# Router logits with tokens on the partitions, and a narrow expert slot first

## The chip, the cores and the metric

The kernel runs on one core of one Trainium2 chip. The metric is the time of one execution on the device in microseconds (us), the median of several runs. Lower is better.

## The reference, cut to what matters

Two layers over 256 tokens of width 1024, in fp32. What the change touches is the end: the output projection of the second layer's attention, the norm, the router and eight experts, of which each token uses two.

```python
x = x + mixer_c(...)                       # ends in o @ w_o
h = rms_norm(x, od_ffn_norm)
logits = h @ router                        # 1024 x 8
top_vals, top_idx = lax.top_k(logits, 2)
w = softmax(top_vals)
for e in range(8):
    out = out + gates[:, e:e+1] * ((silu(h @ e_gate[e]) * (h @ e_up[e])) @ e_down[e])
x = x + out
```

Each expert has three matrices of 1024 x 3584 (or turned) in fp32, 44 MB; all eight are read, 352 MB of the 419 MB that the kernel reads from HBM. 512 pairs of token and expert fall on eight experts. By the reference's inputs the counts are 60, 48, 76, 45, 100, 74, 52, 57.

## The kernel before

The instructions of each engine are written in order by hand, one block for each of PE, ACT, DVE, POOL (GpSimd) and SP, and the engines meet at semaphores.

**Slots.** The expert stage is a sequence of slots, one expert in each. A wide slot takes up to 128 tokens (`CAP`), a narrow one up to 64 (`CAP_N`). The slots run wide, narrow, wide, narrow and so on, eight in all. The first is always expert 0, so that its weights can be loaded before the router has spoken. Of the others, the three with most tokens go into wide slots. An expert with more tokens than its slot holds gets spare slots, added in pairs of wide and narrow, up to `OVER` pairs (`over` is read into registers by all engines).

**Wide slot** (`wide`, 84 quarters of a weight piece each of [128, 1024]). Each quarter is split in two: ACT writes the high part as fp32r (L1379), DVE the rest (L1958), and PE does three fp32r matmuls (`three`, L999 to L1001) for each 512 columns. Splits run four quarters ahead (`AHEAD`). 56 quarters are gate and up, 28 down. Where gate and up meet down, DVE multiplies the two (L1991) and PE turns the hidden values (L880). Toward the end PE turns the next slot's gathered rows (L916).

**Narrow slot** (`narrow`). PE reads the fp32 weights as they lie in the ring, in two column halves of the array (`both`, L932, each matmul recorded as two). Gate and up take 16 pieces, down 8; no splits. Then turns (L926) and turn rows (L852).

**Weights.** SP loads them in pieces of 1.835 MB, 24 to an expert (8 gate, 8 up, 8 down), into a ring of eight places. A place is loaded again when its piece was split (wide, `lo_ready`) or used (narrow, `n_used`). The first piece of the first narrow slot goes to a ninth place, `beside`. The first eight pieces of expert 0 are loaded during the last part of the attention, and then x is stored to `out`.

**Router** (`experts_pe`, `experts_act`, `experts_dve`). The second half of x is complete when DVE has added the last output-projection block (L2123). PE turns x (L1050, L808), ACT and DVE make a gained split transpose (L1324, L1845). PE forms the logits, 8 rows by 256 tokens, in three fp32r passes; DVE copies them out (L1879) and PE turns them (L817). DVE finds the top two (L1890 to L1903), PE counts with triangular and full matrices of ones (L825 to L829), DVE writes the one-hot of expert 0, PE forms its rows already turned (`first_rows`, L838), and ACT and DVE take them over. `idle_matmuls` stand between. The gained rows h are made by DVE (L1859) and stored to `h_rows` by ACT.

**From slot to slot.** During a slot DVE writes the next expert's one-hot, PE turns it into row numbers (`place`, L846), POOL gathers the rows (`exchange`), and after the slot POOL scatters the results, adding to `out`. Before its first exchange POOL sorts the experts into slots (`by_slot`), sets up the spare slots in a loop over `OVER` (L2579 to L2598) and signals `spare_ready`; SP waits for that before it loads a second expert.

Of the kernel before, what the change touches and what calls it, by code (L numbers as in the profile page):

```python
# [54 lines left out]
OVER = 3  # L55
# [24 lines left out]
T_BANK = (6, 7)  # L80
N_BLOCKS = ((0, 512), (512, 512), (1024, 512), (1536, 256))
# [183 lines left out]
def trunk(nc, a, out):  # L265
# [14 lines left out]
    with ExitStack() as ctx:  # L280
# [309 lines left out]
        logitsT = y[0:N_EXP, NW:NW + SEQ]  # L590
        logits_done = sem("logits_done")
        logits_copied = sem("logits_copied")
# [3 lines left out]
        route_ready = sem("route_ready")  # L596
        gain_row_loaded = sem("gain_row_loaded")
# [43 lines left out]
        def is_beside(s, i):  # L641

            return s[0] is None and s[1] == 0 and i == 0
# [11 lines left out]
        def opening(s):  # L655

            return s[0] is None and s[1] == 0

# [16 lines left out]
        def _(sp):  # L675
# [64 lines left out]
            def load_narrow(s):  # L740

                e = sp.value_load(ids[0:1, bass.ds(upto(s, 2, 1), 1)], min_val=0, max_val=N_EXP - 1)
                for i in range(E_PIECES):
                    if is_beside(s, i):
                        load(e, i, beside[:, :], beside_arrived)
                        continue
                    if i < E_RING:
                        sp.wait_ge(lo_ready, upto(s, EQ, split_of_piece(E_PIECES - E_RING + i)))
                    elif is_beside(s, i - E_RING):
                        sp.wait_ge(lo_ready, split_of_piece(E_PIECES - E_RING))  # L750
# [15 lines left out]
            over = sp.value_load(ids[0:1, OVER_AT:OVER_AT + 1], min_val=0, max_val=OVER)  # L766
            sp.wait_ge(spare_ready, 1)
            last = over + (PAIRS - 1)
            for pair in range(PLAIN):
# [14 lines left out]
        def late_bank(k):  # L784

            return bank[(2, 3, 0, 5)[k - KD // 2]]

        def experts_pe(pe, three, turn_norm):
# [7 lines left out]
            def logits(k):  # L796

                pe.wait_ge(hT_lo_ready, 3 * KD + k + 1)
                es = slice(k * N_EXP, (k + 1) * N_EXP)
                return three(bank[4][0:N_EXP, 0:SEQ], aT_hi[:, 0, es], aT_lo[:, 0, es], hT_hi[:, k, :], hT_lo[:, k, :],  # L800
                             k == 0, k == KD - 1)

            for k in range(KD // 2):
                logits(k)
            for t in range(TB):
# [1032 lines left out]
        def experts_dve(dve, projection, split_to, link):  # L1838
# [35 lines left out]
            for k in range(KD):  # L1874
                low(k)
# [783 lines left out]
```

## Time and profile before

| | before |
|---|---|
| median of 3 runs | 1277.42 us (1277.34 to 1278.24) |
| profiled execution | 1278.76 us, span 1276.9 us |
| PE busy | 1216.0 us (95%) |
| DVE, ACT busy | 725.7 us (57%), 663.3 us (52%) |
| read from HBM | 419.06 MB, 332 GB/s over the span |
| mean granted clock of PE | 0.991 of 2.4 GHz |

The span goes from the first to the last instruction. A busy PE is not PE at its peak, as matmuls are pipelined. The expert stage takes the last two thirds of the span. In the chain of work that ended last, PE has 48% and the DMA 11%.

### The profile page before, as it was taken

To read this page: it belongs to the slowest core of one execution; us is meant where nothing else is said; L and a number is where in the kernel's file an instruction comes from. 1 tells how busy PE (TensorE), PEld (TensorE's weight loads), DVE (VectorE), ACT (ScalarE), POOL (GpSimd) and SP (SyncE) were. 2 spreads that over 40 slices of the span, in tenths; PEclk is the share of its full clock that TensorE was granted. 3 is DMA by queue.
4 is the path that set the end of the run, shared out by engine and by line. 5 is a ranking of instruction groups with operands and counts; after the bars stand their busy time and mean duration, and the time that the engine had idled before them with its cause. 6 is when DMAs were issued, how large, how long until landed. Compare 5 with 4: busy or idle time off the path is not lost.

```text
span 1276.9 us, 15629 instructions
## 1 busy us (share of the span) xinstructions
PE 1216.0 (95%) x5885; PEld 842.9 (66%) x5885; DVE 725.7 (57%) x1065; ACT 663.3 (52%) x964; POOL 153.6 (12%) x228
## 2 busy tenths in 40 slices
PE   9989999999989999999899999889999988999997
PEld 7757888888767787843388773348875326878432
DVE  4976555546876889910189950048992007899000
ACT  5676544445796787710278750048772016877100
POOL 0400000000460598010000000010000000000000
PEclk9999999999999999999999999999999998999999
DMA  9804953410635899999999999999999999999995
GB/s 339 308 20 173 357 194 132 149 62 25 247 149 202 314 387 378 363 376 426 427 420 425 428 423 416 426 419 428 427 425 406 428 425 421 426 427 413 389 428 219
DMA packets 62070, 422.98 MB, mean 331 GB/s; under 512 B 5217, under 2 KB 12556, under 8 KB 37420
## 3 DMA queue, kind: packets, MB, share of 16 engines
q1 hardware_dynamic: 59456, 416.40, 80.0%
q0 software_dynamic: 2224, 4.51, 1.5%
q8 instruction: 47, 0.77, 0.2%
q10 hardware_dynamic: 316, 1.07, 0.2%
q14 instruction: 27, 0.22, 0.0%
HBM read 419.06 MB, written 5.24 MB: 332 GB/s over the span
## 4 chain that ended last, share of the span: by engine, by line
PE 48%; DMA 11%; issue 6%; DVE 5%; ACT 1%; POOL 0%; POOLq 0%; SPq 0%; DVEq 0%; ACTq 0%
PE bank L999 12%; PE bank L1001 11%; PE bank L1000 11%; PE bank L932 11%; DMA ring<-in_od_e_gate_dram 7%; DMA ring<-in_od_e_down_dram 4%; DVE w_lo L1958 2%; DVE flat L1991 1%; PE bank L880 1%; DVE aT_lo L1978 0%; DMA out_dram<-h,idx_t 0%; ACT w_hi L1379 0%; PE bank L846 0%; PE bank L838 0%; PE bank L1218 0%
## 5 line engine op out<-in xcount | busy, mean ns | idle before, releaser
L1958 DVE TENSOR_TENSOR w_lo<-ring,w_hi 128x1024 fp32r<-128x1024 f32 x268 | 320.0, 1224 | 54.4 <-ACT w_hi L1379 48.1
L1379 ACT ACTIVATE w_hi<-ring 128x1024 fp32r<-128x1024 f32 x268 | 279.1, 1060 | 81.0 <-PE bank L1001 48.7
L932 PE MATMUL bank<-ring,flat 128*64 128x512 f32 (+1 forms) x1456 | 305.2, 572 | 16.6 <-DMA ring<-in_od_e_down_dram 13.3
L999 PE MATMUL bank<-w_hi,hT_hi 128*128 128x512 f32 (+3 forms) x728 | 282.5, 388 | 11.2 <-DVE w_lo L1958 9.2
L1001 PE MATMUL bank<-w_lo,hT_hi 128*128 128x512 f32 (+3 forms) x728 | 278.3, 382 | 0.0
L1000 PE MATMUL bank<-w_hi,hT_lo 128*128 128x512 f32 (+3 forms) x728 | 278.2, 382 | 0.0
L932 PEld LDWEIGHTS bank<-ring,flat 128*64 128x64 f32 x1456 | 99.0, 135 | 205.5 <-issue 163.4
L2074 DVE TENSOR_TENSOR w_lo<-ring,w_hi 128x1024 fp32r<-128x1024 f32 (+3 forms) x124 | 140.4, 1142 | 83.9 <-ACT w_hi L1491 83.7
L999 PEld LDWEIGHTS bank<-w_hi,hT_hi 128*128 128x128 f32 x728 | 138.4, 190 | 41.2 <-issue 11.0
L1491 ACT ACTIVATE w_hi<-ring 128x1024 fp32r<-128x1024 f32 (+3 forms) x124 | 121.0, 987 | 79.3 <-PE bank L1001 74.9
L1001 PEld LDWEIGHTS bank<-w_lo,hT_hi 128*128 128x128 f32 x728 | 138.2, 190 | 26.4
L1000 PEld LDWEIGHTS bank<-w_hi,hT_lo 128*128 128x128 f32 x728 | 138.5, 190 | 24.8
L999 PE MATMUL bank<-w_hi,aT_hi 128*128 128x512 f32 x306 | 122.3, 400 | 3.2 <-DVE aT_lo L1978 1.8
L1001 PE MATMUL bank<-w_lo,aT_hi 128*128 128x512 f32 x306 | 119.6, 391 | 0.0
L1000 PE MATMUL bank<-w_hi,aT_lo 128*128 128x512 f32 x306 | 119.2, 390 | 0.0
L1434 ACT ACTIVATE flat<-bank 128x512 f32<-128x512 f32 (+1 forms) x16 | 8.7, 544 | 186.6 <-PE bank L926 186.6
L1958 DVE TENSOR_TENSOR hT_lo<-ring,hT_hi 128x1024 fp32r<-128x1024 f32 x64 | 78.2, 1222 | 5.3 <-ACT hT_hi L1379 3.5
L2028 DVE SCALAR_TENSOR_TENSOR flat<-bank,gates,flat 128x512 f32<-128x512 f32 (+1 forms) x16 | 10.5, 682 | 119.1 <-PE bank L932 118.3
L1379 ACT ACTIVATE hT_hi<-ring 128x1024 fp32r<-128x1024 f32 x64 | 67.9, 1060 | 9.7 <-PE bank L1001 9.7
L2611 POOL TENSOR_TENSOR gates<-g_cols 128x1 f32<-128x1 f32 x8 | 3.4, 427 | 557.4 <-ACT h L1419 293.9
L999 PEld LDWEIGHTS bank<-w_hi,aT_hi 128*128 128x128 f32 x306 | 57.6, 188 | 18.3 <-DVE aT_lo L1978 3.8
L1935 DVE TENSOR_TENSOR hT_lo<-bank,hT_hi 128x512 fp32r<-128x512 f32 x10 | 6.5, 686 | 105.7 <-ACT hT_hi L1366 105.7
(363 smaller groups left out, 1216.8 us busy)
## 6 DMA issues: line engine op xcount, KB each, us to landing
ring<-in_od_e_up_dram SPq DMA_DIRECT2D x64, 1792.0 KB, 18.5
ring<-in_od_e_down_dram SPq DMA_DIRECT2D x64, 1792.0 KB, 23.7
ring<-in_od_e_gate_dram SPq DMA_DIRECT2D x63, 1792.0 KB, 17.6
ring<-in_ev_w_gate_dram SPq DMA_DIRECT2D x5, 2048.0 KB, 9.1
ring<-in_ev_w_up_dram SPq DMA_DIRECT2D x5, 2048.0 KB, 13.4
ring<-in_ev_w_down_dram SPq DMA_DIRECT2D x5, 2048.0 KB, 7.6
ring<-in_ev_w_in_dram SPq DMA_DIRECT2D x8, 512.0 KB, 8.7
ring<-in_ev_w_in_dram SPq DMA_DIRECT2D x2, 2048.0 KB, 15.5
```

What stands on the lines that cost most here:

```text
L880: mm = pe.transpose(bank[T_BANK[g % 2]][:, b * P:(b + 1) * P], ye_act[:, at + r:at + HALF_K * P:HALF_K], ident)
L932: mm = pe.matmul(dst[g * CAP_N:(g + 1) * CAP_N, 0:n], left, rights[g], start=first, stop=final)
L999: pe.matmul(dst, hi, whi, start=first, stop=False)
L1000: pe.matmul(dst, lo, whi, start=False, stop=False)
L1001: return pe.matmul(dst, hi, wlo, start=False, stop=final)
L1379: act.activation(e_hi_at[place_of(n)], eights(e_quarter(n)), ACT.Copy).then_inc(hi_ready, 1)
L1434: act.activation(n_actT[:, first * P:(first + tiles) * P], bank[N_T_BANK[g % 2]][:, 0:tiles * P], ACT.Copy).then_inc(n_actT_ready, 1)
L1491: act.activation(w_hi[:, q % SPLITS, 0:m], ring[:, p["place"], at:at + m], ACT.Copy)\
L1958: dve.tensor_tensor(e_lo_at[place_of(n)], eights(e_quarter(n)), e_hi_at[place_of(n)].bitcast(F32), ALU.subtract).then_inc(lo_ready, 1)
L1991: dve.scalar_tensor_tensor(ye_act[:, at], bank[U_BANK[b]][:, :], rinv_cur, ye_act[:, at], ALU.mult, ALU.mult).then_inc(e_hidden, 1)
L2028: dve.scalar_tensor_tensor(n_act[:, at:at + n], bank[4 + b][:, 0:n], rinv_cur, n_act[:, at:at + n], ALU.mult, ALU.mult).then_inc(n_hidden, 1)
L2074: dve.tensor_tensor(w_lo[:, q % SPLITS, 0:m], ring[:, p["place"], at:at + m], w_hi[:, q % SPLITS, 0:m].bitcast(F32), ALU.subtract).then_in ...
```

## The change

Two things. First, the router: the logits are formed with tokens on the partitions, as plain fp32 matmuls of turned x against a router whose rows were multiplied by the gain beforehand (`router_gained`, DVE), so nothing has to be split or turned back. The last block of the output projection is done token block by token block (`o_last_quarter`), with the add and the turning of each behind it. The second half of h is multiplied by the gain on POOL. Some idle matmuls go.

Second, the order of slots: narrow (expert 0), wide, wide, narrow, wide, narrow, wide, narrow. Expert 0 now has the lowest key in the sorting, so the four others with most tokens are wide. `first_rows` forms 64 columns. `beside` now holds piece 8 of the first slot and is loaded once the logits are done. The first wide slot has PSUM banks of its own (`FIRST_BANKS`) and splits four quarters ahead into the second, which waits for `y_ready` before its second quarter. The expert numbers get a signal of their own, `ids_ready`. The spare slots are computed behind POOL's first exchange, with `OVER` 4 and three instructions more in each.

```diff
-OVER = 3
+OVER = 4
+FIRST_BANKS = ((0, 1, 2, 4, 3, 5, 6), (7, 0, 1, 2, 4, 3, 5), (0, 1), (6, 7))
...
         def is_beside(s, i):
-            return s[0] is None and s[1] == 0 and i == 0
+            return s[0] is None and s[1] == 0 and i == E_RING
+        def per_step(s, narrow, more, unit=1):
+            if opening(s):
+                return unit * (more + (0 if narrow else 1))
+            return upto(s, 2 * unit, unit * (more + (1 if narrow else 0)))
...
+                elif i == E_RING:
+                    sp.wait_ge(logits_done, 1)
+                    load(0, i, beside[:, :], beside_arrived)
+                    continue
                 else:
-                    sp.wait_ge(lo_ready, split_of_piece(i - E_RING))
+                    sp.wait_ge(n_used, 1 if i == 2 * E_RING else i - E_RING + 1)
...
+            def load_first_wides():
+                for n in range(2):
+                    e = sp.value_load(ids[0:1, 2 * n:2 * n + 1], min_val=0, max_val=N_EXP - 1)
+                    for i in range(E_PIECES):
+                        if i >= E_RING:
+                            sp.wait_ge(lo_ready, n * EQ + split_of_piece(i - E_RING))
+                        elif n == 0:
+                            sp.wait_ge(n_used, E_PIECES - E_RING + i + 1)
+                        else:
+                            sp.wait_ge(lo_ready, split_of_piece(E_PIECES - E_RING + i))
+                        load(e, i, e_ring(i), e_arrived[i % E_RING])
...
+            sp.wait_ge(ids_ready, 1)
+            load_first_wides()
             sp.wait_ge(spare_ready, 1)
-            for pair in range(PLAIN):
+            for pair in range(1, PLAIN):
...
+            def turn_late(t):
+                pe.wait_ge(hT_hi_ready, 3 * KD + 2)
                 pe.wait_ge(x_added, X_ADDS[3] - TB + t + 1)
                 for k in range(KD // 2, KD):
+                    at = (k - KD // 2) % (4 if t == 0 else 2) * P
+                    b = 2 if t == 0 else (3, 0)[(k - KD // 2) // 2]
+                    mm = pe.transpose(bank[b][:, at:at + P], xres[:, t, k * P:(k + 1) * P], ident)
+                mm.then_inc(hT_turned, 1)
+            def logits(t, ks):
+                for k in ks:
+                    mm = pe.matmul(bank[4][:, SEQ + t * N_EXP:SEQ + (t + 1) * N_EXP],
+                                   xT_all[:, k, t * P:(t + 1) * P],
+                                   router_gained[:, k * N_EXP:(k + 1) * N_EXP], start=(k == 0), stop=(k == KD - 1))
+                return mm
+            turn_late(0)
+            pe.wait_ge(router_ready, 1)
+            logits(0, first_half)
+            turn_late(1)
+            pe.wait_ge(hT_hi_ready, 3 * KD + 3)
+            logits(0, last_half)
+            logits(1, first_half)
+            pe.wait_ge(hT_hi_ready, 3 * KD + 4)
+            pe.wait_ge(hT_lo_ready, 3 * KD + 1)
+            logits(1, last_half).then_inc(logits_done, 1)
-            idle_matmuls(3)
...
-            idle_matmuls(6)
+            idle_matmuls(4)
...
+                        mm = pe.matmul(bank[N_FIRST_BANKS[k // 4]][:, (k % 4) * CAP_N:(k % 4 + 1) * CAP_N],
+                                       h[:, t, k * P:(k + 1) * P], oh[:, t, 0:CAP_N], start=(t == 0), stop=(t == 1))
...
+                    if n == 1 and s[0] is None and s[1] == 1:
+                        pe.wait_ge(y_ready, 2)
...
+                    if i == 2 and opening(s):
+                        pe.wait_ge(slot_ready, 1)
+                        place()
+                    if i == 13 and opening(s):
+                        pe.wait_ge(n_silu, 4)
+                        pe.wait_ge(slot_ready, 2)
+                        place(place_bank(s, True))
...
             first_rows()
+            narrow((None, 0))
             wide((None, 0))
+            wide((None, 1))
...
+                for t in range(TB):
+                    for k in (k0, k0 + 1):
+                        mm = three(o_bank(j, t)[:, :], hT_hi[:, k, rows], hT_lo[:, k, rows], ...)
+                    mm.then_inc(quarter_used if t == TB - 1 else o_block, 1)
...
+            for t in range(TB):
+                pool.wait_ge(x_added, X_ADDS[3] - TB + t + 1)
+                o = pool.tensor_tensor(h[:, t, NW:], xres[:, t, NW:], acf[:, NW:D], ALU.mult)
+            o.then_inc(h_ready, 1)
...
+            pool.tensor_copy(ids[0:1, 0:N_EXP], ids_f[0:1, 0:N_EXP]).then_inc(ids_ready, 1)
...
+            narrow((None, 0))
+            spares()
             wide((None, 0))
+            wide((None, 1))
```

## Rows read from the trace of the kernel before

**Rows 1.** The page, 40 equal slices of the span: throughput of the DMA

```profile
GB/s 339 308 20 173 357 194 132 149 62 25 247 149 202 314 387 378 363 376 426 427 420 425 428 423 416 426 419 428 427 425 406 428 425 421 426 427 413 389 428 219
```

**Rows 2.** Stages: length, busy PE, PEld, DVE, ACT, POOL; clock, DMA share, GB/s

```profile
404.00:428.00 24.00, 20.84 (x125) 16.04 (x125) 14.91 (x48) 15.64 (x33) 1.55 (x2) 1.00 0.98 393
428.00:432.00 4.00, 4.00 (x25) 3.50 (x25) 3.04 (x6) 2.70 (x4) 1.13 (x4) 1.00 0.07 28
432.00:550.00 118.00, 116.73 (x531) 96.20 (x530) 106.24 (x113) 88.64 (x94) 69.56 (x79) 1.00 0.93 364
...
640.00:750.00 110.00, 108.72 (x492) 89.45 (x491) 99.54 (x97) 86.27 (x92) 1.90 (x3) 1.00 1.01 424
```

**Rows 3.** The chain of waits in the expert stage: start us, us, what

```profile
550.74 19.07 PE bank L932 x96
...
570.35 31.68 PE bank L932 x160
602.03 0.70 PE bank L926 x4
602.75 0.61 ACT flat L1434
...
608.17 25.66 DMA ring<-in_od_e_gate_dram
...
636.31 0.47 PE bank L999
...
742.59 0.44 PE bank L916 x4
...
758.99 19.07 PE bank L932 x96
...
848.58 0.76 PE bank L999
```

**Rows 4.** The chain of waits through the router

```profile
412.40 1.28 DVE flat L2123 x2
...
418.58 1.13 DVE w_lo L1852
...
420.47 0.18 DVE route L1890
...
423.01 0.39 PE bank L825 x2
...
424.30 1.47 PE bank L793 x6
425.77 3.57 PE bank L838 x32
429.34 0.30 PE bank L999
```

**Rows 5.** SP's issues of weight pieces behind the first wide slot: start, length, count

```profile
516.13 30.91 SPq L725 DMA_DIRECT2D ring<-in_od_e_gate_dram  x7
```

**Rows 6.** PE by time in the last narrow slot

```profile
1241.21 6.23 PE L932 MATMUL bank<-ring,flat 128*64 128x512 f32 x28
...
1262.40 1.09 PE L852 MATMUL bank<-cst,h 128*128 128x128 f32 x8
```

**Rows 7.** POOL: a group by line (busy, mean ns), then instructions by time

```profile
L2475 POOL TENSOR_TENSOR ring<-ring,rinv 128x512 f32<-128x512 f32 x2 | 4.0, 2032 | 37.1 <-DVE rinv L2161 37.1
...
433.49 12.64 POOL L2555 TENSOR_TENSOR kr<-cnt,cst 128x32 f32<-128x32 f32 x2 [4.22 <-DVE ids L1954]
...
460.56 1.08 POOL L2579 TENSOR_TENSOR route<-route,cnt 128x16 f32<-128x16 f32 x1
...
467.80 0.19 POOL L2586 COPY pos_t<-cst 128x2 f32<-128x2 f32 x1
...
507.13 0.18 POOL L2608 TENSOR_TENSOR gates<-g_cols 128x1 f32<-128x1 f32 x1
...
564.95 0.18 POOL L2617 TENSOR_TENSOR idx_t<-idx_t 128x1 uint32<-128x1 uint32 x1 [10.37 <-DMA out_dram<-h,idx_t]
```

More of the change, by code:

```diff
@@ L867, in quarter @@
                         half = slice(k % 8 * P, (k % 8 + 1) * P)
-                        mm = three(out(D_BANK[b]), eT_hi[:, half], eT_lo[:, half], wh, wl, k == 0, k == 2 * HALF_K - 1)
+                        mm = three(out(d_bank[b]), eT_hi[:, half], eT_lo[:, half], wh, wl, k == 0, k == 2 * HALF_K - 1)
                     else:
-                        mm = three(out((G_BANK if kind == "gate" else U_BANK)[b]), hT_hi[:, k, 0:CAP], hT_lo[:, k, 0:CAP],
+                        mm = three(out((g_bank if kind == "gate" else u_bank)[b]), hT_hi[:, k, 0:CAP], hT_lo[:, k, 0:CAP],
                                    wh, wl, k == 0, b in ended_banks(kind, n))
@@ L984, in experts_pe @@
             last = over + (PAIRS - 1)
-            for pair in range(PLAIN):
+            for pair in range(1, PLAIN):
                 narrow((None, pair))
@@ L1361, in experts_act, with take_gathered @@
             o.then_inc(e_once, 1)
-            def take_gathered(first):
+            def take_gathered(first, banks):
                 for m in range(2):
@@ L1452, in experts_act @@
             last = over + (PAIRS - 1)
-            for pair in range(PLAIN):
+            for pair in range(1, PLAIN):
                 narrow((None, pair), (None, pair + 1))
@@ L1985, in wide @@
                         split(s, n + AHEAD)
+                    if n + AHEAD >= EQ and opening(s):
+                        split((None, 1), n + AHEAD - EQ)
                     if ended:
@@ L2033, in narrow @@
                         split(after, n)
+            dve.wait_ge(placed, 1)
+            take_halves_placed()
+            narrow((None, 0), (None, 0))
             wide((None, 0))
+            wide((None, 1))
             dve.wait_ge(route_ready, 1)
@@ L2038, in experts_dve @@
             last = over + (PAIRS - 1)
-            for pair in range(PLAIN):
+            for pair in range(1, PLAIN):
                 narrow((None, pair), (None, pair + 1))
@@ L2608, in exchange @@
+            def exchange(s, narrow, dst, rows, to, results):
+                pool.wait_ge(idx_ready, per_step(s, narrow, 2))
+                pool.wait_ge(rows_turned, per_step(s, narrow, 1, 2))
                 pool.tensor_tensor(seen_rows, g_cols[:, 0:1], g_cols[:, 0:1], ALU.add)
                 gather(dst, rows)
[L2610 removed]
+                pool.wait_ge(y_ready, per_step(s, narrow, 1))
                 pool.tensor_tensor(seen_y, g_cols[:, 0:1], g_cols[:, 0:1], ALU.add)
@@ L2614, in exchange @@
                     .then_inc(scattered, 16)
-                pool.wait_ge(gathered, upto(s, 32, 16 * (slot + 1)))
-                pool.wait_ge(scattered, upto(s, 32, 16 * (slot + 1)))
+                pool.wait_ge(gathered, per_step(s, narrow, 1, 16))
+                pool.wait_ge(scattered, per_step(s, narrow, 1, 16))
                 pool.tensor_tensor(idx_cur, idx_next, zero_u, ALU.add).then_inc(idx_taken, 1)
             def wide(s):
-                exchange(s, 0, he[:, 0:NW], h_halves, out[0], ye)
+                if opening(s):
+                    exchange(s, False, he, h_rows, out[0], ye)
+                else:
+                    exchange(s, False, he[:, 0:NW], h_halves, out[0], ye)
             def narrow(s):
-                exchange(s, 1, he, h_rows, out_halves, ye[:, 0:NW])
+                exchange(s, True, he, h_rows, out_halves, ye[:, 0:NW])
             last = over + (PAIRS - 1)
+            narrow((None, 0))
+            spares()
             wide((None, 0))
-            for pair in range(PLAIN):
+            wide((None, 1))
+            for pair in range(1, PLAIN):
                 narrow((None, pair))
```

393 lines of the change are left out of this document (203 added, 190 removed).

## The prediction

> **What bounds the kernel now.** I read the throughput of the DMA by slices first [rows 1]. From the nineteenth slice on (575 us) they move 406 to 428 GB/s, save one of 389 and the last; in the five before (415 to 575) it is 314 to 387. So the expert stage streams weights at a ceiling, except in its first 150 us. Then I cut it into stages [rows 2]. In the 118 us of the first wide slot (432 to 550) the DMA engines are busy for 0.93 and move 364 GB/s; in the later wide slot (640 to 750) 1.01 and 424 GB/s. Just before the stage, from 404 to 428, they run at 393 GB/s to fill the ring, and from 428 to 432 they stand nearly still (28 GB/s): the ring of eight pieces is full and nobody has emptied a place.
>
> The chain of waits gives the slots [rows 3]. Narrow slot: PE begins at 550.74, does gate and up in 19.07 + 31.68 us, and at its end waits 25.66 us for a gate piece. The next wide slot begins at 636.31 and ends at 758.99 (122.7 us); the one after begins at 848.58. A pair, wide and narrow, thus takes 212.3 us for 48 pieces of 1.835 MB: 4.42 us a piece, including the gathers and scatters. The first wide slot runs from 429.34 [rows 4] to 550.74, 121.4 us. So a wide slot consumes a piece in 5.1 us, slower than the DMA delivers, and a narrow slot could consume one in 3.4 us (below). In the steady state the wide slot's surplus of 19 us is eaten by the narrow slot and the DMA sets the pace. At the start it isn't: the ring is full, the wide slot doesn't empty it fast enough, and the issues on SP's queue come every 5.1 us [rows 5], the splits' pace.
>
> The page "DMA: Bandwidth & Descriptors" of the Trainium skill (Where 436 GB/s comes from) says that loads from HBM are bound at about 358 GB/s, below the fabric's 435. By that a piece would take 5.13 us, a wide slot would never fall behind the DMA, and the order of slots would bring nothing. This trace disagrees: 424 GB/s over 110 us [rows 2]. The sums below use the 4.42 us.
>
> **The change, part by part.**
>
> *Router.* Before, DVE adds the two halves of x at 412.40; its routing starts at 420.47, 8.07 us later; from there the first wide slot is 8.87 us away [rows 4]. After, DVE adds token block 0 under the matmuls of block 1, so one add (0.64) remains after 412.4, and transposes of four blocks cost 0.5 (eight of 128x128 took 1.09 [rows 6]). Logits become fp32 matmuls with 8 columns; the nearest row is the count matmul, 0.22 us each for 5 of them between 423.01 and 424.30 with the first at 0.39 [rows 4]. PE: transposes to 412.85, four logits matmuls to 413.75, transposes of block 1 to 414.2, eight more to 416.0 over the copies on ACT and DVE (a copy of 512 columns on ACT took 0.61 [rows 3], these have half), the last four to 416.9. The hT_lo passes, the first split (1.13) on DVE, the copy and the transposes of the logits leave the path. Routing starts at 417.0: 3.5 us gained. With matmuls at 0.39 instead of 0.22 it would be about 1 us later by the last four alone and about 2.5 by all; without any wait between, 0.5 earlier. I take 3.5.
>
> From routing to the first product: 2.54 for the masks and 1.3 for the counts stay. The idle matmuls after them go from six (1.47) to four (1.0): 0.5 gained. DVE's compares, which fitted under six, must fit under 1.0; if they don't, at most the 0.5 comes back. The gained half of h moves from DVE to POOL: two products of 128x512. POOL's nearest rows take 2.0 us [rows 7]; 412.4 + 0.64 + 2 x 2.0 is 417, against 420 when the compares need it. Hidden; if it weren't, each us is a us. First rows stay 16 products in 3.57 with half the columns: the count matmuls with 8 columns also take 0.22, so the width brings nothing (upper gain 1.8). The first slot begins at 429.34 - 3.5 - 0.5 = 425.3.
>
> *DMA at the start.* The piece `beside` (index 8) is issued once the logits are done, at about 417. The five gate pieces, x and h keep the DMA busy to 428 [rows 2]; the ninth piece extends that to 432.3. SP then waits for two used pieces. A narrow slot's gate piece takes 50.75/16 = 3.17 us, so that is 425.3 + 6.3 = 431.6: the DMA has at most 2 us of gap. From about 433.8 piece k lands at 433.8 + 4.42 (k - 8).
>
> *First narrow slot.* Gate and up 50.75; two placements 1.1 (0.54 each, from 550.74 + 19.07 to 570.35 [rows 3]); down 112 recorded matmuls at 6.23/28 = 0.2225 [rows 6], 24.9; turning 14 blocks at 0.70 for four, 2.5; the copy of the first turned ones 0.6 [rows 3]; turn rows 1.1. Sum 81.0: to 506.3. Arrival: piece 23 is due at 500.1 and used from about 503, so PE isn't starved, by 3 us. Piece 24 lands at 504.5; with the 2.5 us from landing to first product (608.17 + 25.66 to 636.31) the wide slot can begin at 507.0. I take 507.0.
>
> *Two wide slots.* Each 121.4, as the first of before (its splits were ahead too; the other row is 122.7). Between them PE needs the first slot's results copied out of two banks, after one quarter (1.4 us) of work; two copies of 0.6 on ACT. I take 0.5 us; nothing if the copies win, 4 if the split pipeline must restart. W2 ends at 507.0 + 121.4 + 0.5 + 121.4 = 750.3. The ring fills again: piece 72 would land at 716.7, and its place comes free 82 us into the slot at about 711, so for the last 40 us of W2 the DMA is held to 5.1 us a piece, just as before at the end of its first wide slot.
>
> *Rest.* From the end of W2 everything is as after the first wide slot of before: 85.57 us to the next wide slot (550.74 to 636.31), at 835.9. There the ring had one piece more (`beside`), but SP waited for two used pieces instead of one; that cancels within 1 us. Before, the same wide slot (the third) began at 848.58. Gain 12.7; with 0.7 us from the earlier reissue of the first freed place, 13.4. What follows is unchanged and bound by the DMA.
>
> *POOL and the queues.* The spare computation leaves the start and comes after the first scatter. In the trace the three spares take 39.3 us (467.80 to 507.13) plus 7.2 of preparation [rows 7]. Four with two or three more instructions each: about 15 us x 4 + 7 = 67. The scatter is over 14.2 us after a slot's end (550.74 to 564.95), so the spares run from 520 to 587, and the gather lands at 597. PE wants it 106 us into W1 (742.59 less 636.31) = 613. Hidden by 16 us. SP's wide loads wait for `ids_ready` at 476; even with the 12.64 us that the first two instructions took in the trace it is there by 456. The splits that stood ahead of the first slot are done during the narrow slot, where DVE has nothing else.
>
> **Sum.** 1276.9 - 13.4 = 1263.5 for the span; with the 1.9 us between span and time of the profiled run (1278.76) 1265.4. The profiled run lay 1.34 above the median 1277.42, so the forecast for the median is 1264.0.
>
> **Rivals.**
>
> *A, as forecast*, chance 0.68: 1260 to 1268.
>
> *B, narrow slot starved*, 0.14: the DMA is less than 3 us ahead of PE in the first narrow slot. If it starts late or the narrow slot takes the 85.57 us of every later one, W1 begins 4 to 8 us later, and nothing gives that back, since two PE-bound slots follow: 1268 to 1272. For it: the deliveries late in narrow slots do lag. Against it: there the ring started nearly empty.
>
> *C, the clock*, 0.06: three idle matmuls go and six become four. The granted clock was 1.00 throughout 404 to 428 in spite of 3.2 us of idle PE in that window [rows 2]. If it fell to half for the first rows (3.57 more) and the first us of the slot, 4 to 6 us: 1268 to 1270.
>
> *D, no gain*, 0.05: both A's PE chain and the DMA lose, by a restart of the splits between the wide slots (4), a starved narrow slot (5) and a router no earlier (4). 1277.
>
> *E, slower*, 0.04: the spares on POOL. They have 16 us of slack; each instruction waits its turn with DVE. If they take t us more than 67, the gather stalls W1 by t - 16 and W2 after it. From t = 32 the change is slower than before; at twice the time (134), 51 us stall, 1264 + 51 = 1315. Against it: DVE was as busy when the three took 13.1 each. The page "SBUF — State Buffer" of the Trainium skill (Who interferes with whom) says that a DVE instruction with two SBUF inputs and a GpSimd one that reads SBUF block each other for a whole instruction. The first wide slot bore about 70 of them in 121.4 us, no more than the 122.7 of one without.
>
> *F, it doesn't do what it says*, 0.03: the first slot is narrow whatever the load. With over 64 tokens on expert 0 a spare pair is added, 212 us: 1476. The reference's inputs give expert 0 sixty tokens, and the smallest gap between second and third logit (0.003) is far above fp32 error; the four other slots hold.
>
> **Range and chances.** The ends take A and B and the unknown costs: below, first rows at half the width (1.8), no waits between logits (0.5) and a shorter narrow slot, 1259; above, B, 1272. Less than 0.2 lies outside. A measurement tells 0.2% (2.6 us) from no change. Faster takes A, B, C and small parts of D: 0.89; same 0.05; slower 0.06.
>
> **What would show it.** Routing starts near 417; the first product on a ring piece near 425; the wide slots at about 507 and 628, narrow at 750, wide at 836. DMA above 415 GB/s from 433 to 710, then about 370 to 750. In the first narrow slot no wait for a down piece over 2 us; W1 without a wait for `gathered`. The prediction is wrong if the time from 425 to W1 is over 85 us, if the second wide slot starts with a gap, or if the gather of W1 lands after 613.

## The result, and the profile after

| | before | after |
|---|---|---|
| median, lowest and highest of 20 runs | 1277.57 (1276.69 to 1279.69) us | 1270.2 (1267.9 to 1279.42) us |
| ratio to before, 95% interval | | 0.995 (0.9939 to 0.9961) |
| span of the profiled execution | 1276.9 us | 1269.6 us |

The change is faster by 7.4 us by the medians (0.6%) and by 6.4 by the ratio (0.5%). The forecast was 1264.0 us, a gain of 13.4, so about half of it came. The median lies inside the stated 1259 to 1272, but above the 1260 to 1268 of the forecast's own case A and in the stretch that was given to rivals B (a starved narrow slot) and C (the clock). The span came out 6.1 us above its forecast of 1263.5. The changed kernel also scatters more: 11.5 us between its lowest and highest run, against 3.0 before.

The throughput of the DMA in 40 slices, on the page of the changed kernel, answers to [rows 1]:

```profile
GB/s 336 310 25 165 366 199 133 149 63 25 222 177 169 376 428 425 420 427 427 426 415 401 357 338 416 427 419 428 427 427 414 428 427 420 427 426 421 395 427 220
```

The five weak slices from 415 to 575 us have become one (376). The hole is not gone: three slices of 401, 357 and 338 stand from 667 to 762 us, at the end of the second wide slot. The same by stages, as [rows 2] (length, busy PE, PEld, DVE, ACT, POOL; granted clock, DMA share, GB/s):

```profile
414.00:416.00 2.00, 2.00 (x18) 2.00 (x17) 0.65 (x4) 1.91 (x7) 0.62 (x5) 0.83 1.02 437
416.00:418.00 2.00, 2.00 (x9) 1.98 (x10) 0.21 (x2) 1.66 (x3) 0.00 (x0) 0.50 1.07 445
418.00:420.00 2.00, 2.00 (x6) 1.53 (x5) 1.73 (x11) 0.00 (x0) 0.00 (x0) 0.50 0.93 389
420.00:422.00 2.00, 2.00 (x8) 1.61 (x7) 0.42 (x3) 0.00 (x0) 0.00 (x0) 0.50 1.07 440
422.00:424.00 2.00, 2.00 (x13) 1.59 (x13) 0.88 (x8) 0.05 (x1) 0.00 (x0) 0.96 0.98 411
432.00:434.00 2.00, 2.00 (x14) 0.69 (x12) 0.00 (x0) 0.00 (x0) 0.00 (x0) 1.00 0.24 94
434.00:440.00 6.00, 6.00 (x32) 2.25 (x30) 0.98 (x6) 0.20 (x1) 1.37 (x6) 1.00 0.82 301
440.00:510.00 70.00, 68.09 (x338) 24.67 (x334) 5.08 (x9) 7.71 (x13) 1.34 (x2) 1.00 1.01 425
510.00:600.00 90.00, 87.08 (x382) 70.42 (x383) 80.41 (x80) 69.79 (x75) 63.52 (x88) 1.00 1.01 424
640.00:710.00 70.00, 70.00 (x312) 57.86 (x310) 62.67 (x60) 57.01 (x59) 2.19 (x3) 1.00 0.98 394
710.00:755.00 45.00, 43.72 (x205) 35.84 (x205) 39.42 (x43) 29.55 (x33) 0.00 (x0) 1.00 0.93 362
```

Two things to see. The granted clock falls from 2.4 to 1.2 GHz between 415 and 416 and is back at about 422, and PE is busy 2.00 of 2.00 us all that time; in the kernel before the clock was 1.00 throughout [rows 2]. And after the start of the narrow slot the DMA has a gap: 94 GB/s for 2 us and 301 for 6. Against 424 that is 2 x (1 - 94/424) + 6 x (1 - 301/424) = 3.3 us of delivery lost.

The chain of waits (start us, us, what), as [rows 3, 4]:

```profile
414.02 3.63 PE bank L872 x24
417.65 4.04 PE bank L856 x9
421.92 0.39 PE bank L894 x2
...
424.00 3.69 PE bank L906 x32
427.68 9.62 PE bank L1003 x48
...
509.05 30.16 DMA ring<-in_od_e_gate_dram
539.23 1.07 ACT w_hi L1469
...
755.72 19.07 PE bank L1003 x96
...
813.15 26.61 DMA ring<-in_od_e_gate_dram
...
842.25 0.77 PE bank L1086
```

L872 are the logits, L856 idle matmuls, L894 the first counts, L906 the first rows, L1003 the narrow slots' products, L1086 the first of the three passes of a wide slot. PE begins the narrow slot at 427.68. Between the logits and the counts stand nine idle matmuls, and they outlast what they were to bridge: DVE's last mask, for which the counts wait, is done at 420.45. In the kernel before the nine took 2.33 us. First the mask after, then the nine before:

```profile
420.28 0.17 DVE L1978 TENSOR_SCALAR route<-route 128x16 f32<-128x16 f32 x1
```

```profile
420.30 2.33 PE L793 MATMUL bank<-aT_hi 128*128 128x512 f32 x9
```

The next long link is a transfer: a gate piece of the first wide slot issued at 509.05 lands 30.16 us later, and only then can ACT split it. PE's own timeline shows where that wide slot begins (the bracket is idle time before, and who ended it), and the waits of ACT in 500 to 650 us what it waited for (total, times, longest):

```profile
510.44 0.47 PE L1086 MATMUL bank<-w_hi,hT_hi 128*128 128x512 f32 x1 [1.58 <-DVE w_lo L2030]
```

```profile
ACT w_hi L1469 <- DMA ring<-in_od_e_gate_dram: 13.0, 7, 4.6
```

In its first wide slot the kernel before has no wait of ACT on the DMA. SP's queue in the changed kernel:

```profile
417.68 0.33 SPq L770 DMA_DIRECT2D beside<-in_od_e_up_dram  x1
434.19 19.93 SPq L770 DMA_DIRECT2D ring<-in_od_e_up_dram  x7
...
675.74 33.25 SPq L770 DMA_DIRECT2D ring<-in_od_e_down_dram  x8
717.09 0.33 SPq L770 DMA_DIRECT2D ring<-in_od_e_gate_dram  x1
```

After the ninth place (417.68) nothing is issued until two pieces have been used, 434.19.

### The profile page after: what moved, and what is told of

It reads as the page before. It is cut to its first block, busy times and chain, and to the rows that moved or that the text cites. A ratio compares the mean times of both kernels' runs of the same rounds, so it can differ in the third digit from the quotient of the medians.

```text
span 1269.6 us, 15658 instructions
## 1 busy us (share of the span) xinstructions
PE 1215.0 (96%) x5890; PEld 844.5 (67%) x5890; DVE 720.3 (57%) x1055; ACT 661.0 (52%) x960; POOL 152.5 (12%) x256
## 4 chain that ended last, share of the span: by engine, by line
PE 50%; DMA 9%; issue 6%; DVE 5%; ACT 1%; POOL 0%; POOLq 0%; DVEq 0%; SPq 0%; ACTq 0%
PE bank L1003 14%; PE bank L1086 11%; PE bank L1088 11%; PE bank L1087 10%; DMA ring<-in_od_e_gate_dram 7%; DVE w_lo L2030 2%; DMA ring<-in_od_e_down_dram 2%; DVE flat L2073 1%; PE bank L949 1%; DVE aT_lo L2058 0%; PE bank L856 0%; DMA out_dram<-h,idx_t 0%; PE bank L872 0%; PE bank L914 0%; PE bank L997 0%
## 5 line engine op out<-in xcount | busy, mean ns | idle before, releaser
L2030 DVE TENSOR_TENSOR w_lo<-ring,w_hi 128x1024 fp32r<-128x1024 f32 x272 | 323.6, 1221 | 54.9 <-ACT w_hi L1469 48.9
L1469 ACT ACTIVATE w_hi<-ring 128x1024 fp32r<-128x1024 f32 x272 | 282.2, 1059 | 80.9 <-PE bank L1088 43.4
L1003 PE MATMUL bank<-ring,flat 128*64 128x512 f32 (+1 forms) x1456 | 304.1, 570 | 14.2 <-DMA ring<-in_od_e_down_dram 11.1
L1086 PE MATMUL bank<-w_hi,hT_hi 128*128 128x512 f32 (+3 forms) x728 | 281.4, 387 | 9.4 <-DVE w_lo L2030 7.7
L1003 PEld LDWEIGHTS bank<-ring,flat 128*64 128x64 f32 x1456 | 98.7, 135 | 201.8 <-issue 163.7
L1086 PEld LDWEIGHTS bank<-w_hi,hT_hi 128*128 128x128 f32 x728 | 137.7, 189 | 40.4 <-issue 9.9
L1086 PE MATMUL bank<-w_hi,aT_hi 128*128 128x512 f32 x306 | 122.5, 400 | 3.4 <-DVE aT_lo L2058 2.1
L1086 PEld LDWEIGHTS bank<-w_hi,aT_hi 128*128 128x128 f32 x306 | 57.6, 188 | 18.9 <-DVE aT_lo L2058 4.5
L1088 PEld LDWEIGHTS bank<-w_lo,aT_hi 128*128 128x128 f32 x306 | 57.4, 188 | 12.4
L1087 PEld LDWEIGHTS bank<-w_hi,aT_lo 128*128 128x128 f32 x306 | 57.6, 188 | 11.0
```

The lines of the kernel that those rows point to most:

```text
L1003: mm = pe.matmul(dst[g * CAP_N:(g + 1) * CAP_N, 0:n], left, rights[g], start=first, stop=final)
L1086: pe.matmul(dst, hi, whi, start=first, stop=False)
L1087: pe.matmul(dst, lo, whi, start=False, stop=False)
L1088: return pe.matmul(dst, hi, wlo, start=False, stop=final)
L1469: act.activation(e_hi_at[place_of(n)], eights(e_quarter(n)), ACT.Copy).then_inc(hi_ready, 1)
L2030: dve.tensor_tensor(e_lo_at[place_of(n)], eights(e_quarter(n)), e_hi_at[place_of(n)].bitcast(F32), ALU.subtract).then_inc(lo_ready, 1)
```

## The experiments

Each is compared with the kernel before on the same chip; its median there was 1277.79 to 1278.24 us, given where a difference is formed. "After" is the changed kernel.

### The router without the order

The kernel before with only the new router (turning by token block, fp32 logits, the gain on POOL):

```diff
-            for k in range(KD // 2, KD):
-                mm = logits(k)
...
+            turn_late(0)
...
+            logits(0, first_half)
+            turn_late(1)
...
+            logits(0, last_half)
+            logits(1, first_half)
...
+            logits(1, last_half).then_inc(logits_done, 1)
```

> The kernel before with the new router alone: logits with tokens on the partitions, the last output-projection block by token blocks, h on POOL, fewer idle matmuls; slots as before, wide first, and the first two splits on ACT and DVE fitted in while the logits are formed. Theory 1 (the router's work brings 1.7 us, from 429.34 to 427.7 in the first product on a weight piece, and the slot order the rest of 7.3): the median is 1 to 3 us under the kernel before, the first wide slot begins at about 427.5 and ends at about 549. Rival (the order brings nothing here and the router all): 6 to 8 us under. Rival 2 (the start doesn't matter, as the DMA sets the pace): within 0.5 us.

Measured: 1275.02 us, ratio 0.998 (0.9971 to 0.9989), 2.9 us below 1277.88. In the profiled execution the clock fell here too, and stayed low longer:

```profile
418.00:420.00 2.00, 2.00 (x8) 1.53 (x7) 1.73 (x11) 1.99 (x4) 0.00 (x0) 0.61 1.01 401
420.00:428.00 8.00, 8.00 (x33) 7.23 (x32) 3.15 (x16) 2.64 (x5) 1.82 (x5) 0.50 0.98 401
```

The first rows took 5.46 us (3.57 before) and nothing of the router's gain was left in that execution, the longest of the eleven: the first wide slot began at 430.31 and ended at 551.66, where about 427.5 and 549 were expected and the kernel before had 429.34 and 550.74. The median came out as expected, the path to it didn't. The fall of the clock belongs to the router, not to the order, since it occurs with the old order too. By the difference of the medians the order of slots brought the other 4.5 of 7.4 us, where the forecast had 4.0 from the router and 9.4 from the order.

### Logits over 64 columns

Is it the narrow products that let the clock fall? Each of the 16 logits matmuls streams 64 columns instead of 8; the gained router stands twice, and only the first 8 columns of each result are used.

```diff
+        W_L = KD * N_EXP
...
-                    mm = pe.matmul(bank[4][:, SEQ + t * N_EXP:SEQ + (t + 1) * N_EXP],
+                    mm = pe.matmul(bank[4][:, SEQ + t * W_L:SEQ + (t + 1) * W_L],
...
-                                   router_gained[:, k * N_EXP:(k + 1) * N_EXP], start=(k == 0), stop=(k == KD - 1))
+                                   router_gained[:, k * N_EXP:k * N_EXP + W_L], start=(k == 0), stop=(k == KD - 1))
```

> The changed kernel with logits matmuls that stream 64 columns instead of 8: the gained router is written twice side by side, each product takes the 64 columns that begin with its own 8, and only the first 8 results of each block are read. PE has the same number of instructions. Theory 1 (the small products let the clock fall, and the clock, not the length of the router, is what the router's 2.4 us went to): the granted clock stays at or near 1.00 from 412 to 430, the first product on a weight piece comes within 13.6 us of the last output-projection matmul (15.4 in the changed kernel), the runs scatter less, and the median falls by 1.5 to 4 us. Rival (the clock falls for another reason, the wait around 411 or the idle matmuls' place): nothing changes, within 0.5 us.

Measured: 1270.15 us (1269.4 to 1271.56), ratio 0.994 (0.9927 to 0.9954). Stages and chain:

```profile
416.00:418.00 2.00, 2.00 (x11) 1.62 (x10) 1.47 (x9) 1.25 (x2) 0.00 (x0) 1.00 1.08 453
418.00:420.00 2.00, 1.48 (x12) 1.13 (x11) 0.89 (x6) 0.00 (x0) 0.00 (x0) 1.00 0.97 395
```

```profile
413.59 2.64 PE bank L873 x24
...
418.87 0.39 PE bank L894 x2
...
421.18 3.68 PE bank L907 x32
424.86 9.62 PE bank L1004 x48
```

The clock stays at 1.00, the last twelve logits matmuls take 2.64 us instead of 3.63, and PE begins the narrow slot at 424.86, where the prediction had 425.3. All steps of the router were right but for the clock. The clock was held in the other two kernels with 64 columns and the new order as well, which follow below. Yet the median hardly moves, where 1.5 to 4 us were expected: the profiled span is 2.2 us shorter (1267.4), the median the same as after's. The runs do scatter less, 2.2 us between the lowest and the highest of five. One reading, not tested by itself, is that after's executions scatter with the length of the slow clock and its median one loses less than the profiled one. And part of the 2.8 us is lost again at once, as PE now waits 2.18 us (after: 1.58) before the wide slot's first product, at 508.22. The DMA's gap after the start of the narrow slot is smaller than after's, but still there:

```profile
432.00:434.00 2.00, 2.00 (x12) 0.69 (x10) 0.00 (x0) 0.00 (x0) 0.00 (x0) 1.00 0.86 208
434.00:440.00 6.00, 6.00 (x36) 2.33 (x32) 0.98 (x6) 0.20 (x1) 1.38 (x6) 1.00 1.00 406
```

With 352 GB/s in the 2 us before, that is 1.6 us of delivery lost, against 3.3.

The same on the kernel with only the router:

> The kernel before with the new router alone, and its logits with 64 columns streamed instead of 8. Slots as before. Theory 1 (the new router is worth 4 us at full clock, and the earlier run with 8 columns lost most of that because its clock was at half from 418 to 430): the granted clock stays at 1.00, the first product of the first wide slot comes 4 us earlier relative to the end of the output projection, and the median is 3 to 4.5 us under the kernel before. Rival (what the router gains, the DMA takes back, since the ring isn't full before 428): under 2 us.

Measured: 1274.85 us, ratio 0.997 (0.996 to 0.9981), 3.4 us below 1278.24; the wide slot ended at 547.97, 2.8 earlier than before. The median is where it was expected (3 to 4.5), but here the clock wasn't held, and the first product of the first wide slot came 2.8 us earlier and not 4. Four windows of 2 us from 418 had 1.00, 0.74, 0.50 and 0.91, and the first rows took 4.94 us. In the first of these PE was busy for 1.22 us; in the kernel with the new order it had 1.48 and kept its clock. The two edits differ in one more thing: with the old order a split on DVE stands between the logits and the routing. Over all profiled executions with the new router, the clock fell in six of six with 8 columns and in one of four with 64. So 64 columns make the fall rarer or shorter; they don't exclude it.

### Idle matmuls among the logits, and before the first rows

```diff
             logits(0, first_half)
+            idle_matmuls(2)
             turn_late(1)
...
             logits(0, last_half)
+            idle_matmuls(2)
```

> The changed kernel with two idle matmuls of 512 columns behind the first four logits matmuls and two behind the third four. In the changed kernel the granted clock was 0.83 from 414 to 416 and 0.50 from 416 to 422, and nine idle matmuls took 4.04 us where they took 2.33 before. Theory 1 (the matmuls with 8 columns cost the clock, and that holds back the counts): the clock stays at 1.00, the counts start at about 420.6 instead of 421.9, the first product at about 426.4 instead of 427.7, and the time falls by 1 to 1.5 us against the changed kernel. Rival (the clock falls anyway, on account of the wait of PE around 412): the logits are 1 us later and the time rises by 0 to 1 us.

Measured: 1272.37 us, ratio 0.9952 (0.9937 to 0.9966). The clock fell all the same, only later (0.64 in 418 to 420, 0.50 in 420 to 422), and the first product came at 428.30 and not at 426.4. The median is 2.2 us above after's (1.9 when each is taken against the kernel before on its own chip), more than the 0 to 1 of the rival. The idle matmuls cost their time and bought nothing.

How does a delay at the start go through to the end? 26 idle matmuls stand before the first rows instead of four:

```diff
-            idle_matmuls(4)
+            idle_matmuls(26)
```

> The changed kernel with 26 idle matmuls instead of 4 ahead of the first rows, 22 x 0.2275 = 5.0 us more before the first slot. Theory 1 (PE's chain, narrow, wide, wide, sets when the ring gets going, 1 to 1): 4.5 to 5.5 us slower than the changed kernel. But the DMA would have more time to land the pieces for the start of the first wide slot, which gives back up to 2: then 3 to 4.5. Rival (the DMA sets the end from the start on): under 1 us.

Measured: 1274.71 us, ratio 0.998 (0.9969 to 0.999), 4.5 above after's median (4.2 when each is taken against the kernel before on its own chip). In the profiled execution the 26 took 6.04 us, but its clock was back earlier, so the first product came at 430.51, 2.8 later than after. The second wide slot ended 3.0 later, the third began at 845.50, 3.25 later, and the span is 2.7 longer. So a microsecond at the start was about a microsecond at the end: up to the end of the second wide slot PE sets the pace, and the later stages keep the distance.

### The freed place first

SP waits for two used pieces before it issues piece 9, and behind it stands piece 16, whose place (that of piece 0) is free after one. Here piece 16 goes first.

```diff
-            for i in range(E_PIECES):
+            for i in [*range(E_RING + 1), 2 * E_RING, *range(E_RING + 1, 2 * E_RING), *range(2 * E_RING + 1, E_PIECES)]:
```

> The changed kernel with one difference in SP's order: piece 16, whose place is free after one used piece, is issued ahead of piece 9, which needs two. In the changed kernel the DMA engines stood at a share of 0.24 from 432 to 434 and 0.82 from 434 to 440. Theory 1 (the second slot starts late and runs 2.7 us long because pieces land late in the first slot and a half): the gap closes, piece 24 lands some 2.5 us earlier than 507.9, and the time falls by 1.5 to 3 us against the changed kernel. Rival (PE's chain alone sets the end, since the narrow slot ended at 508.9 anyway): less than 1 us.

Measured alone: 1271.58 us (1267.37 to 1275.64), ratio 0.9942 (0.992 to 0.9964), not to be told from after; the 1.5 to 3 us that were expected aren't seen. Its six runs fall in two groups, 1267.4 to 1268.4 and 1274.8 to 1275.6, and the profiled one is of the second: there the clock was low from 416 to about 436, PE began only at 431.45, and the DMA moved 98 GB/s in 434 to 440. So it says nothing on the start. But PE went from narrow to wide at 514.94 without a wait, ACT waited only 5.0 us for gate pieces, and the two wide slots took 244.0 us together (after: 755.72 - 510.44 = 245.3). The faster group, about 7 us below the slower, is what one would see if the clock fell for long in half of the runs; the mean clock of the runs (0.986 to 0.992 in the faster group, 0.986 to 0.988 in the slower) doesn't settle it.

With 64 columns as well:

> The last kernel, and piece 16 issued ahead of piece 9. Theory 1 (both losses are real and add up): 2 to 3.5 us less than with 64 columns alone, as ACT no longer waits for gate pieces in the first wide slot (13.0 us of waits in the changed kernel) and the two wide slots together take 244 us instead of 245.3, starting within 0.2 us of the narrow slot's end instead of 1.6. Rival (the earlier issue only helped because the clock had delayed PE): the waits stay and it is within 0.5 us.

Measured: 1268.06 us, ratio 0.9932 (0.9918 to 0.9945), 2.1 below the kernel with 64 columns alone (ratio 0.994, 0.9927 to 0.9954: the intervals overlap, so the times alone don't show it); span 1264.5, 2.9 shorter. Stages and PE's timeline:

```profile
432.00:434.00 2.00, 2.00 (x12) 0.68 (x10) 0.00 (x0) 0.00 (x0) 0.00 (x0) 1.00 1.05 445
434.00:440.00 6.00, 6.00 (x36) 2.30 (x32) 0.98 (x6) 0.20 (x1) 1.37 (x6) 1.00 1.01 428
```

```profile
505.93 0.50 PE L1087 MATMUL bank<-w_hi,hT_hi 128*128 128x512 f32 x1
```

The gap of the DMA is closed, the wait of 2.18 us before the wide slot is gone, and its second wide slot ends at 751.05, where the prediction had 750.3. The other half of the expectation failed: ACT still waited 10.5 us for gate pieces (11.3 with 64 columns alone), and the two wide slots took 245.1 us, no less than after's. Apart from the length of that pair this is the execution that was forecast: clock held, DMA without a gap, and a span 1.0 above the 1263.5.

### Without the third pass

What does the full ring in the wide slots still cost? `two` leaves out the product of the low part of the weights with the high part of the rows, in the first two wide slots; places then come free faster.

```diff
+            def two(dst, hi, lo, whi, wlo, first, final):
+                pe.matmul(dst, hi, whi, start=first, stop=False)
+                return pe.matmul(dst, lo, whi, start=False, stop=final)
...
+                product3 = two if s[0] is None and s[1] < 2 else three
```

> The changed kernel with the third pass (high times low part of the weights) left out in the first two wide slots, so PE has 38 us less work in each; the splits on ACT and DVE stay, so a slot can shrink to about 111 us. Theory 1 (two wide slots in a row are slower than the DMA and the full ring costs it about 10 us): the third wide slot begins 11 to 14 us earlier than 842.25, as the DMA then runs without a gap, and the time falls by 11 to 14 us against the changed kernel. Rival (the DMA's own rate between 434 and 842 is the limit): under 4 us.

Measured: 1262.76 us (1258.57 to 1266.0), ratio 0.9869 (0.9852 to 0.9885), 7.4 below after by the medians and 10.3 by the ratios. The stage that had the hole:

```profile
640.00:755.00 115.00, 101.20 (x403) 65.90 (x403) 96.25 (x100) 83.15 (x92) 23.00 (x7) 0.94 1.01 420
```

420 GB/s to the end of the slots, against 394 and then 362. The start and the chain behind the slots:

```profile
432.00:434.00 2.00, 2.00 (x6) 0.46 (x4) 0.00 (x0) 0.15 (x1) 0.00 (x0) 0.50 0.14 57
434.00:440.00 6.00, 6.00 (x26) 1.93 (x24) 0.00 (x0) 0.00 (x0) 0.00 (x0) 0.80 0.01 3
```

```profile
742.88 19.07 PE bank L1009 x96
...
804.68 28.74 DMA ring<-in_od_e_gate_dram
...
835.90 0.77 PE bank L1092
```

The second narrow slot began at 742.88, 12.8 us earlier than after, but the third wide slot only at 835.90, 6.4 earlier and not the 11 to 14 that were expected: the stretch between them grew from 86.5 to 93.0 us, with PE waiting for pieces. Part of the miss is the clock, which was low until about 436 in this execution, so that PE emptied the first place late. From 432 to 440 the DMA lost 2 x (1 - 57/424) + 6 x (1 - 3/424) = 7.7 us of delivery, 4.4 more than after; that this is the missing part is an estimate and not a measurement. With no full ring in these slots the DMA sets the time, and that is worth 7 to 10 us here.

The kernel before with the same in its first wide slot alone:

> The kernel before with the third pass left out in its first wide slot alone. Theory 1 (in that kernel the full ring costs the DMA over 20 us, all of it by the length of the first wide slot, 1 to 1): the slot takes about 111 us instead of 121.4 and the whole 9 to 11 us less. Rival (the DMA sets the pace from the start): under 2 us.

Measured: 1272.45 us, ratio 0.9955 (0.9942 to 0.9969), 5.3 below 1277.79. A miss. The slot ended only 7.2 us earlier (at 543.58; it had begun 0.6 later). PE now stands idle between its products, above all until DVE has a split ready, and its granted clock is 0.91 from 440 to 520; how much each of the two costs isn't separated. The DMA moved no more than this:

```profile
432.00:550.00 118.00, 102.77 (x400) 67.48 (x401) 103.99 (x115) 88.34 (x98) 74.49 (x81) 0.94 0.95 378
```

378 GB/s instead of 364 is 118 x 14/424 = 3.9 us of DMA won back in this stage. Where PE's work goes and the splits stay, the slot shows little of what the DMA could do. The changed order doesn't have this limit in the narrow slot, which has no splits.

### The ninth place used again

After the second wide slot the prediction let a missing ninth place and a shorter wait of SP cancel. Here, on top of the kernel with 64 columns and the freed place first, the ninth place takes piece 0 of the second narrow slot too:

```diff
-            return s[0] is None and s[1] == 0 and i == E_RING
+            return s[0] is None and (s[1], i) in ((0, E_RING), (1, 0))
```

> The kernel with 64 columns and piece 16 first, and the ninth place used a second time, for the first piece of the second narrow slot, as the kernel before did at the end of its first wide slot. The piece behind it can then be issued before the second wide slot ends and not 3.3 us after. Theory 1 (the missing place at that point is the 1.6 us by which the second narrow slot and its wait came out longer than forecast, 86.6 us instead of 85): that stretch shrinks by 1 to 3 us and so does the time, against 1268.06 of the kernel without it (ratio 0.9932). Rival (the DMA has enough in its queue there): within 0.5 us.

Measured: 1266.45 us (1265.13 to 1267.59), ratio 0.9908 (0.9893 to 0.9924), the fastest kernel with the reference's full work; span 1263.9. Chain and SP's queue:

```profile
751.40 19.07 PE bank L1010 x96
...
808.84 25.18 DMA ring<-in_od_e_gate_dram
...
836.50 0.47 PE bank L1093
```

```profile
705.46 0.33 SPq L772 DMA_DIRECT2D beside<-in_od_e_gate_dram  x1
716.80 30.91 SPq L772 DMA_DIRECT2D ring<-in_od_e_gate_dram  x7
747.81 30.04 SPq L772 DMA_DIRECT2D ring<-in_od_e_up_dram  x8
```

The first gate piece leaves at 705.46, where it was 712.43 in the kernel that this one is built on (717.09 after). From the end of the second wide slot to the third it takes 85.1 us, against 86.6 in that kernel, 86.5 after and 85.57 before [rows 3]. So the two didn't cancel: 1.4 us of the 1.6 that this stage was over its forecast come from the ninth place. Of that 0.6 is left in the span against the kernel that it was built on (1264.5); the medians are 1.6 apart (1268.06 and 1266.45), with intervals of the ratios that overlap a little (from 0.9918 to 0.9924).

## Why the prediction was right in kind and off in size

| step | forecast | after | off by |
|---|---|---|---|
| first product of the narrow slot | 425.3 | 427.68 | +2.4 |
| narrow slot | 81.0 | 81.2 | +0.2 |
| from its end to the first wide slot | 0.7 | 1.56 | +0.9 |
| two wide slots | 243.3 | 245.3 | +2.0 |
| to the third wide slot | 84.9 | 86.5 | +1.6 |
| from there to the end | 428.3 | 427.3 | -1.0 |

The sum is 6.1, the whole of the span's error. The mechanism held: PE sets the pace up to the end of the second wide slot, the DMA from there on. What failed are the terms of the sum below. With the logits at 64 columns, the freed place first and the ninth place used again, the span was 1263.9, 0.4 above the forecast; part of that closeness is luck, since terms of both signs are left in it.

That the median fell in rival B's 1268 to 1272 is no point for B, whose mechanism isn't what happened, and C's 1268 to 1270 is near it for another reason than C gave.

**Routing and the clock.** Routing was to start at 417.0 and came at 417.76. The step that failed is "From routing to the first product: 2.54 for the masks and 1.3 for the counts stay", together with rival C's place in it. It took for granted that the nine idle matmuls ahead of the counts stay hidden under the masks, as before, where they took 2.33 us of the 2.54. At half the clock they took 4.04: the masks were ready at 420.45, 2.7 us after routing had started, and the counts began only at 421.69. The term behind it, "from six (1.47) to four (1.0): 0.5 gained", held (1.01). C put the fall on the missing idle matmuls and on the first rows, at 4 to 6 us and a chance of 0.06. It came earlier, while PE had no idle time, during the fp32 logits matmuls of 8 columns, and it cost 2.4 us in the profiled execution: from the end of the output projection to the first product it took 15.38 us (412.30 to 427.68), and with 64 columns 12.99 (411.87 to 424.86). Of this 1.0 is in the last twelve logits (3.63 against 2.64), most of the rest in the nine idle matmuls. With 64 columns the term is 424.86 against 425.3: right to 0.4. Which executions fall for 4 to 6 us and which for 20 is open; that this is what scatters the times is likely and not shown. That the few columns are the cause is supported by three profiled executions with the new order and 64 columns (all at 1.00 up to the first rows) and weakened by the one with the old order (0.74 and 0.50 in spite of 64). Why they should let the clock fall no run shows.

**The start of the DMA.** "The DMA has at most 2 us of gap" was mis-sized: 3.3 us of delivery were lost, since the first product came 2.4 later and SP waits for two pieces (issue at 434.19, not 431.6). With the clock held the loss was 1.6 us, inside the 2, with the issue at 431.37. The step that failed even so is "the wide slot can begin at 507.0", a wait of 0.7 us behind the narrow slot: it was 1.56 after and 2.18 with 64 columns, where the slot began at 508.22. It was not the narrow slot that starved, as rival B has it (it took 81.2 us), but the wide slot's splits behind it: B's mechanism one stage later. Issuing the freed place first takes this wait away, as the trace with 64 columns shows (505.93).

**Two wide slots.** 243.3 was mis-sized by 2.0. The boundary between them was right: PE goes over with a gap of about 0.2 us. The first slot took 124.1, the second 121.2. The pair took 244.0 in the one execution in which ACT waited only 5.0 us for gate pieces, and 245.1 to 246.8 in the others with all three passes, in which it waited 10.5 to 13.2 us. So up to 1.3 us may belong to pieces that land late; with the freed place first and 64 columns nothing of it came back. The cause of the 2.0 stays open.

**The ring full again** was forecast for the last 40 us of the second wide slot at about 370 GB/s; it is 362 in the last 45, and 394 in the 70 before. Leaving out the third pass shows that this holds 7 to 10 us of the whole. The page "DMA: Bandwidth & Descriptors" of the Trainium skill (Where 436 GB/s comes from) gives about 358 GB/s as the bound from HBM. The trace after the change disagrees as the one before did: 425 GB/s over 70 us in the narrow slot.

**After the second wide slot** "that cancels within 1 us" failed: +1.6, of which the ninth place gives back 1.4. The rest of the kernel, unchanged, was 1.0 us shorter than before; nothing tested says why.

**POOL** (rival E, 0.04) was no issue, as forecast. The spares ran from 524 to 588, 64 us for a forecast of 67, and nobody waited for `gathered` in the first wide slot. Nor do they slow DVE. The splits of the first wide slot, with POOL busy for 63.5 of 90 us, and those of the second, with POOL at 2.2 of 70 (min/median/max ns, start times):

```profile
L2030 DVE TENSOR_TENSOR w_lo<-ring,w_hi x69: 1207/1221/1250, 511.8 to 633.0; 128x1024 fp32r<-128x1024 f32 x69
L2030 DVE TENSOR_TENSOR w_lo<-ring,w_hi x66: 1208/1224/1227, 633.0 to 749.2; 128x1024 fp32r<-128x1024 f32 x66
```

It is POOL that pays. DVE had no split from 537.54 to 540.32, while ACT waited for a gate piece, and the same small instruction of POOL took a fifth of the time there:

```profile
536.54 1.06 POOL L2593 TENSOR_TENSOR route<-route 128x8 f32<-128x8 f32 x1
...
539.04 0.20 POOL L2593 TENSOR_TENSOR route<-route 128x8 f32<-128x8 f32 x1
```

The page "SBUF — State Buffer" of the Trainium skill (Who interferes with whom) says that a DVE instruction with two SBUF inputs contends with a GpSimd instruction that reads SBUF. The trace agrees for POOL (0.20 and 1.06 us) and shows nothing of it on DVE (medians of 1221 and 1224 ns). Rivals D and F didn't occur.

Of the signs that were named ahead, the gap between the wide slots, the 85 us from 425 to the first wide slot (82.8) and the late gather didn't occur. "DMA above 415 GB/s from 433 to 710" failed at both ends: 301 up to 440, and 394 from 640 on.

## What to carry to other kernels

Where one engine sets the pace through several stages, each microsecond lost before them is a microsecond of the result, so read the granted clock beside the busy share: a full busy column doesn't mean a full clock. When a stage of short matmuls takes the place of long ones, try streams with as many columns as cost nothing extra. Where idle matmuls bridge a wait, price them at half the clock too: they stand in PE's queue ahead of the work. And where a queue waits for the second of two things to start the first, look for an entry behind it that could go already: here one line of order took away a wait of 2.18 us, and a ring place put to use gave 1.4 in its stage.

## What the hardware showed that was not expected

- The granted clock fell to 0.50 for 6 us (416 to 422), and in other executions to about 428 or 436, with PE busy 2.00 in every window of 2 us. Up to the fall, or to within about 1 us of it, the work was fp32 matmuls of 8 columns.
- At full clock twelve such matmuls (24 records) took 2.58 us with 8 columns (the kernel with 26 idle matmuls) and 2.64 with 64. Eight times the columns are nearly free.
- A weight piece of 1.8 MB took 30.16 us from issue to landing, with the DMA at 424 GB/s; at 4.42 us a piece that is the time of 6.8 pieces, so by this estimate about seven, itself included, were on their way.
- POOL's first two small instructions behind the expert numbers took 21.73 us beside busy splits in one kernel (before with two passes in its first wide slot), 12.64 in the kernel before, and 0.44 after, where DVE has no splits at that time.
